# Attention in pairs of heads, with the stick-breaking weights from the sigmoid table

## The reference

```python
def nsa_compressed(q, kc, vc, slopes):       # 31 compressed keys
    ...
    p = jax.nn.softmax(s, axis=-1)
    p = jnp.where(valid.any(-1)[:, None], p, 0.0)
    o = jnp.einsum('bgrqn,bgnd->bgrqd', p.astype(vc.dtype), vc)
    return o, p.sum(axis=2)

def nsa_selected(...)   # s = q.k * scale - slope * dist, causal, softmax, times v
def nsa_window(...)     # the same with other keys and values

def stick_breaking(q, k, v):
    ...
        z = jnp.einsum('bhqd,bhkd->bhqk', qq.astype(jnp.float32), kf) * ATTN_SCALE
        log_keep = jnp.where(mask, -jax.nn.softplus(z), 0.0)
        later = lax.cumsum(log_keep, axis=3, reverse=True) - log_keep
        a = jnp.where(mask, jnp.exp(jax.nn.log_sigmoid(z) + later), 0.0)
        return jnp.einsum('bhqk,bhkd->bhqd', a.astype(v.dtype), v)

    o_a = g_a[..., 0:1] * o_cmp + g_a[..., 1:2] * o_sel + g_a[..., 2:3] * o_win
    y_a = o_a.transpose(0, 3, 1, 2, 4).reshape(B, S, NSA_Q_DIM) @ w_proj_a
    y_b = o_b.transpose(0, 2, 1, 3).reshape(B, S, SB_HEADS * hd) @ w_proj_b
    y = jax.nn.sigmoid(merge[:, :, 0]) * y_a + jax.nn.sigmoid(merge[:, :, 1]) * y_b
    return y @ w_out
```

## Time and profile before

| | us |
|---|---|
| median of 3 runs (2045.61 to 2047.15) | 2045.71 |
| profiled execution, its own time | 2046.02 |
| its span | 2044.3 |
| stage_compress, first instruction | 201.1 |
| attention's first instruction, first score | 264.9, 269.05 |
| first product of the merge | 435.53 |
| PE busy over the span | 1806.7 (88%) |
| DVE, ACT, POOL busy over the span | 819.3, 516.2, 36.1 |

### The profile page before, as it was taken

One profiled execution on the slowest core, in us unless ns is written; L12 is line 12 of the kernel. 1 busy time (PEld: TensorE's weight loads), 2 busy tenths in 40 slices (PEclk: granted clock), 3 DMA queues, 4 the chain that ended last, 5 costly groups with the idle time before them and its releaser, 6 DMA issues. The chain is left out here.

```text
span 2044.3 us, 20691 instructions
## 1 busy us (share of the span) xinstructions
PE 1806.7 (88%) x8271; PEld 1284.3 (63%) x8271; DVE 819.3 (40%) x1346; ACT 516.2 (25%) x873; POOL 36.1 (2%) x59
## 2 busy tenths in 40 slices
PE   6899779989987999999959989998899888888865
PEld 6788667766666888878848876757333343343344
DVE  1663388852225223233452274333423332322344
ACT  3312156641123222222243242322200000000032
POOL 0000000000000000000000000000200000000000
PEclk9899579999988999999979999999999999999977
DMA  8565100022331232230422111225599999999901
GB/s 330 178 242 182 43 1 1 1 83 70 136 124 41 84 123 83 87 120 21 165 72 83 42 42 41 83 115 240 193 427 424 427 427 426 427 427 427 424 18 41
DMA packets 93434, 353.71 MB, mean 173 GB/s; under 512 B 8813, under 2 KB 50457, under 8 KB 77593
## 3 DMA queue, kind: packets, MB, share of 16 engines
q1 hardware_dynamic: 90778, 343.98, 43.1%
q0 software_dynamic: 2560, 8.40, 1.1%
HBM read 343.93 MB, written 6.33 MB: 171 GB/s over the span
## 5 line engine op out<-in xcount | busy, mean ns | idle before, releaser
L549 PE MATMUL up_ps<-up_h,up_w 128*128 128x512 f32 x352 | 137.8, 391 | 5.7 <-DVE up_h L544 5.7
L544 DVE TENSOR_TENSOR p_w<-ring,p_w 128x1024 fp32r<-128x1024 f32 x60 | 73.5, 1224 | 167.1 <-ACT p_w L589 167.0
L550 PE MATMUL up_ps<-up_h,up_w 128*128 128x512 f32 x352 | 137.5, 391 | 0.0
L551 PE MATMUL up_ps<-up_h,up_w 128*128 128x512 f32 x352 | 137.4, 390 | 0.0
L2272 PE MATMUL ex_h<-ring,u_big_tail 128*64 128x512 f32 x512 | 116.6, 603 | 13.1 <-DMA ring<-in_w 12.5
L2272 PE MATMUL ex_h<-s_ab,u_big_tail 128*64 128x512 f32 x400 | 114.7, 596 | 12.6 <-DMA s_ab<-in_w 5.5
L589 ACT CAST p_w<-ring 128x1024 fp32r<-128x1024 f32 x60 | 62.8, 1047 | 128.7 <-PE p_ps L551 86.8
L2243 DVE TENSOR_TENSOR u_big_tail<-ex_x,vcol 128x512 f32<-128x512 f32 x32 | 20.6, 686 | 184.9 <-PE ex_x L2236 184.9
L544 DVE TENSOR_TENSOR up_w<-ring,up_w 128x1024 fp32r<-128x1024 f32 x44 | 53.9, 1226 | 87.1 <-ACT up_w L589 87.1
L2272 PEld LDWEIGHTS ex_h<-ring,u_big_tail 128*64 128x64 f32 x512 | 39.5, 138 | 76.0 <-issue 74.9
L2477 ACT ACTIVATE u_big_tail<-ex_h 128x512 f32<-128x512 f32 x16 | 9.6, 597 | 305.7 <-PE ex_h L2272 305.7
(11 more groups left out here) (484 smaller groups left out, 3772.2 us busy)
## 6 DMA issues: line engine op xcount, KB each, us to landing
ring<-in_w SPq DMA_DIRECT2D x48, 2048.0 KB, 28.8
s_ab<-in_w SPq DMA_DIRECT2D x36, 2048.0 KB, 28.3
ring<-in_w_in SPq DMA_DIRECT2D x15, 2048.0 KB, 9.0
reg_a<-in_w SPq DMA_DIRECT2D x12, 2048.0 KB, 32.4
ring<-in_w_ada SPq DMA_DIRECT2D x16, 1024.0 KB, 4.7
ring<-in_w_ffn_gate SPq DMA_DIRECT2D x11, 1024.0 KB, 5.2
ring<-in_w_ffn_up SPq DMA_DIRECT2D x11, 1024.0 KB, 7.8
ring<-in_w_ffn_down SPq DMA_DIRECT2D x5, 2048.0 KB, 7.7
```

What stands on the lines that cost most here:

```text
L544: return engine.tensor_tensor(lo, v, hi.bitcast(F32), ALU.subtract)
L549: nc.tensor.matmul(ps, x[0], y[0], start=start, stop=False)
L550: nc.tensor.matmul(ps, x[0], y[1], start=False, stop=False)
L551: return nc.tensor.matmul(ps, x[1], y[0], start=False, stop=stop)
```

## The change

Units become steps over pairs of heads: (block t, pair n, kind), first four stick pairs of a block, then eight softmax pairs, 48 in all. The query isn't spread any more: each head of the pair is a product over its own 64 rows. Each step's two heads lie in one buffer of two banks, `ps_s[i % 2]`, are copied in one instruction, and there is one transpose buffer `ps_t` of two banks. The stick weights are made from Sigmoid(-z), what is kept: ACT writes it (L1181), POOL writes 1 on and above the diagonal (L1226), DVE scans products from the right (L1150) and subtracts neighbours (L1153). The values are now the fixed operand (64 columns) and the turned weights move, so the outputs come with features on the partitions, head 2n in the lower and 2n+1 in the upper half; ACT copies them (L1187, L1191). Since tokens now lie along the columns, the factors of a block are widened by POOL (L1234), turned by eight products (L1099) in the next block's sixth step (`block_end(s, 6)`), copied by ACT (L1198), and DVE multiplies and adds (L1168 to L1170) into `b.qT`, from which the merge reads. The stick result goes into `b.sqT`. The turning stage is empty, and the reload of `b.reg_a` is issued at the attention's start. In stage_compress `b.sbmask` goes, `cs` is scaled by `cfac` before it is turned, and the product with the values is four products of 512 columns, copied by DVE and ACT in turn.

```diff
@@ stage_compress
-            nc.gpsimd.memset(b.sbmask, 0.0).then_inc(pool, 1)
-            pe.wait_ge(expd, 1)
+            pe.wait_ge(shared, 1)
...
-            for t in range(NT):
-                pe.wait_ge(pte, t // 2 + 1)
-                for g in range(2):
-                    mm = nc.tensor.matmul(ps_o[t][:, g * REP * HD:(g + 1) * REP * HD], pTc[:, t, g, :], vbd[:, g, :], ...)
+            pe.wait_ge(pte, 2)
+            for n in range(4):
+                nc.tensor.matmul(ps_o[n][:], vbd[:, n // 2, n % 2 * P:n % 2 * P + P], pTc[:, :, n // 2, :],
+                                 start=True, stop=True).then_inc(o, 1)
...
+            nc.vector.tensor_tensor(cs, cs, cfac.unsqueeze(3).to_broadcast([P, NT, HEADS, NC]), ALU.mult).then_inc(shared, 1)
@@ stage_attention
-    PER = 3 * HEADS
-    units = [(t, i // 3, i % 3) for t in range(NT) for i in range(PER)]
+    PER = 12
+    units = [(t, n, kind) for t in range(NT) for kinds in ((2,), (0, 1)) for n in range(4) for kind in kinds]
+        @block.sync
+            sp.dma_start(b.reg_a[:], b.h_dram).then_inc(b.h_back, 16)
         @block.tensor
+            def turn(i):      # waits p_stick or p_soft, and copied >= i
+                for e in range(2):
+                    for c in range(t + 1):
+                        mm = nc.tensor.transpose(ps_t[:, e, c * P:c * P + P], buf(i)[:, e, c * P:c * P + P], b.ident[:])
+                mm.then_inc(pt_ready, 1)
+            def values(i):    # waits copied >= i + 1
+                for c in range(t + 1):
+                    for e in range(2):
+                        mm = nc.tensor.matmul(ps_o[n % 2][64 * e:64 * e + 64, 0, kind * P:kind * P + P], v,
+                                              turned[i % 2][:, e, c * P:c * P + P], start=(c == 0), stop=(c == t))
+                    for e in range(2):
+                        r, k = slice(64 * e, 64 * e + 64), (t + 1) * P
+                        q = (b.sqT if kind == 2 else b.qT)[r, n, t * P:t * P + P]
+                        ks = b.skT[r, n, 0:k] if kind == 2 else b.kk[kind][r, n // 2, 0:k]
+                        nc.tensor.matmul(ps_s[i % 2][:, e, 0:k], q, ks, start=True, stop=True).then_inc(scored, 1)
+                if t is not None:                       # block_end(s, 6)
+                    pe.wait_ge(widened, 2 * t + 2)
+                    for kind in range(2):
+                        for n in range(4):
+                            mm = nc.tensor.matmul(ps_t[:, kind, n * P:n * P + P], wide[kind][:, n * P:n * P + P], b.ident[:], ...)
+                    mm.then_inc(spread, 1)
+                    values(at(s, 4)); pe.wait_ge(shared, t + 1); turn(at(s, 3))
+                else:
+                    turn(at(s, 3)); values(at(s, 4))
         @block.vector
+                    for e in range(2):                  # softmax pair, at its step
+                        nc.vector.tensor_tensor_reduce(out=buf(i)[:, e, 0:k], in0=ps_s[i % 2][:, e, 0:k], in1=b.bias[...], ...)
+                    for e in range(2):                  # stick pair, one step later
+                        last = nc.vector.tensor_tensor_scan(out=left[:, e, 0:k][:, ::-1], data0=w[:, e, 0:k][:, ::-1],
+                                                            data1=zero.to_broadcast([P, k]), initial=1.0, op0=ALU.mult, op1=ALU.add)
+                    nc.vector.tensor_tensor(w[:, :, 0:k], left[:, :, 1:k + 1], left[:, :, 0:k], ALU.subtract).then_inc(p_stick, 1)
+                    link(nc.vector.tensor_tensor(raw, raw, shares..., ALU.mult))      # block_end(s, 7)
+                    link(nc.vector.tensor_tensor(raw[:, 0], raw[:, 0], raw[:, 1], ALU.add))
+                    nc.vector.tensor_tensor(b.qT[:, :, q], raw[:, 0], b.oa[:, :, q], ALU.add).then_inc(y_made, 1)
         @block.scalar                                   # in this order within a step s
+                    nc.scalar.activation(buf(i)[:, :, 0:k], ps_s[i % 2][:, :, 0:k], ACT.Sigmoid, scale=-1.0)   # stick pair s
+                    last = nc.scalar.copy(b.sqT... or raw..., ps_o[n % 2]...)                                  # pair s - 5
+                    nc.scalar.copy(shares, ps_t[:]).then_inc(shared, 1)                                        # block_end(s, 6)
+                    nc.scalar.copy(turned[i % 2][:, :, 0:k], ps_t[:, :, 0:k]).then_inc(copied, 1)              # pair s - 3
+                    for e in range(2): nc.scalar.activation(buf(i)[:, e, 0:k], ..., ACT.Exp, ..., accum_out=...)  # softmax pair s
         @block.gpsimd
+                    nc.gpsimd.affine_select(out=own, in_=own, compare_op=ALU.is_gt, fill=1.0, base=0, ...)
+                        nc.gpsimd.tensor_copy(wide[kind]..., fac[:, :, kind].unsqueeze(2).to_broadcast([P, HEADS, HD]))
@@ stage_turn
+    return
```

More of the change, by code:

```diff
@@ L1024, in stage_attention, with pair @@
[L1024 to L1031 removed]
+    def pair(reg, u0):
+        return reg[:, u0 * U:(u0 + 2) * U].rearrange("p (e k) -> p e k", e=2)
@@ new lines, in stage_attention @@
+    turned = [pair(b.hTflat, 4 + 2 * i) for i in range(2)]
+    share = [pair(b.w1flat, 2 * i) for i in range(3)] + [pair(b.hTflat, 2 * i) for i in range(2)]
+    raw = b.w1flat[:, 6 * U:8 * U].rearrange("p (b n q) -> p b n q", b=2, n=4)
+    left = b.scr[:, 0:2 * U + 2].rearrange("p (e k) -> p e k", e=2)
+    wide = [b.scr[:, 2 * U + 2:3 * U + 2], b.u_big[:, 8 * U:9 * U]]
+    shares = pair(b.s_b, 4)
+    negm = b.small[:, 0:4].rearrange("p (i e) -> p i e", i=2)
+    fac = b.small[:, 24:40].rearrange("p (h b) -> p h b", b=2)
@@ new lines, in stage_attention, with stick, block_end, buf @@
+    first = [i for i in range(N) if units[i][2] != 1]
+    def stick(i):
+        return i is not None and units[i][2] == 2
+    def block_end(s, lag):
+        t = (s - lag + 1) // PER - 1
+        return t if (s - lag + 1) % PER == 0 and 0 <= t < NT else None
+    def buf(i):
+        return share[i % 5]
+    with ExitStack() as ps_ctx:
+        def banks(n, k):
+            return ps_ctx.enter_context(nc.psum_tensor(f"at_{n}", [P, k, CH], F32))
+        ps_s = [banks(f"s{i}", 2) for i in range(2)]
+        ps_t = banks("t", 2)
+        ps_o = [banks(f"o{i}", 1) for i in range(2)]
@@ L1077, in _ @@
[L1077 to L1087 removed]
+                    t, n, kind = units[i]
@@ new lines, in _ @@
+                i = at(s, 0)
+                if i is not None and not stick(i):
+                    t, n, kind = units[i]
+                    k, m = (t + 1) * P, softs.index(i)
+                    if t >= 2 and n == 0:
+                        act.wait_ge(fac_made, t - 1)
+                    for e in range(2):
+                        act.wait_ge(taken, 2 * m + e + 1)
+                        last = nc.scalar.activation(buf(i)[:, e, 0:k], buf(i)[:, e, 0:k], ACT.Exp, scale=-1.0,
+                                                    bias=negm[:, m % 2, e:e + 1], accum_out=b.rows2[:, t % 2, 2 * n + e, kind:kind + 1])
+                    last.then_inc(p_soft, 1)
```

346 lines of the change are left out of this document (139 added, 207 removed).

## The result

| | before | after |
|---|---|---|
| median, us | 2045.66 (2044.92 to 2047.15, 4 runs) | 2015.35 (2013.52 to 2018.86, 4 runs) |
| profiled span, us | 2044.3 | 2011.8 |
| first score of the attention | 269.05 | 269.65 |
| first product of the merge | 435.53 | 406.23 |
| between the two | 166.5 | 136.6 |

The account below looks back on a forecast made before the run. TensorE was taken to bound blocks t = 2 and 3. 267.5 + 117.0 + 7.5 + 1.5 + 15, + 2.5 - 0.5, put the merge at 410.5 against 435.5: 25 us less, 2045.7 to 2020.7 us, range 2005 to 2039.

Parts of the forecast that it names:

- PE's sum per step: Attention, PE's work per pair step with row halves at once: 1.20, 1.86, 2.51, 3.17 us for t = 0 to 3.
- The steps taken: Attention steps including waits between engines: 1.65, 2.15, 2.65 and 3.3 us, times 12 is 117.0 us.
- No successor to the stops: Block ends: PE's three old stops, 10.8 us in all, vanish; spreading the factors adds 2.5 us each, 7.5 us.
- t = 0: First attention block: ACT bounds it at 1.42 us a step, taken as 1.65; low clock at the start adds 1.5 us.
- First score: Attention's start: zeroing and copies go (-4.1 us), stage_compress grows; first score between 266 and 269.3, taken as 267.5 us.
- Tail: After the last step: transposes, copies, values, spreading, DVE steps and barrier take 15 us, where it was 20.
- Merge: Merge's first 3.7 us of products run at half speed for part of the time after PE idles: +2.5 us.
- (a): Rival, attention scores: row halves run one after the other, some 22 us more, 2043 us; chance 0.09.
- (b): Rival, softmax steps: PE's transposes, ACT's copy and two Exp follow without overlap, +14 us, 2034 us; chance 0.11.
- (c): Rival, attention: clock stays at 1.2 GHz because of PE's gaps, 47 us more if through t = 2, 2068; chance 0.06.
- (d): Rival, attention steps: everything overlaps as PE's sum alone, 12 us less, 2009 us; chance 0.08.
- (e): Rival, ACT: two heads in one instruction may cost more than one long row; ends in the ACT copy-loop rival, 2034.

Follow-up runs that it names:

- run 1: Changed kernel with both heads' score products reading the same upper 64 rows of queries and keys: 2038.93 us, ratio to before 0.9961.
- run 2: Changed kernel with transposes and value products reordered by head, adding two changes of shape in a step: 2028.57 us, 150.8 us from score to merge.
- run 6: Changed kernel with an exponential in place of the sigmoid, so no table loads within the attention: 127.9 us from score to merge; total 2364.12 us differs by its data.
- run 4: Changed kernel with five unread products of 512 columns on PE before the attention: 2010.94 us, ratio 0.9824, 136.4 us from score to merge.
- run 5: Kernel before the change, without DVE's wide steps at each block's end: 146.4 us from score to merge against 166.5; total 2094.0 us says nothing.
- run 11: Changed kernel with POOL's mask cut to 4 of 128 columns per head: 2084.88 us (differs by its data), 137.1 us from score to merge, single run.

## Why the prediction was right, point by point

2020.7 was forecast, 2015.35 measured; 25 us of gain, 30.3 measured. The main step, PE's sum with row halves at once, is right and shown. The total is closer than the parts deserve, by errors of opposite sign.

- *PE's sum per step*, 0.65(t+1) + 0.55, holds to 0.06 us: 1.86, 2.51, 3.17 against 1.81, 2.46, 3.11. Row halves at once: right (run 1). The switches, 0.55 a step from two gaps of the earlier trace rows, are 0.51, and 0.15 each when added (run 2). Two sums are a little off on paper: 120 records in 7.1 us are 0.059 each and not 0.055 (0.055 is their spacing inside that stretch), and 0.65 x 4 + 0.55 is 3.15, not 3.17.
- *The steps taken*, 2.15, 2.65, 3.3, added 0.13 to 0.29 for waits between engines. There are none in a steady step. That alone is 12 x (0.34 + 0.19 + 0.19) = 8.6 us too much.
- *"No successor to the stops" and table loads in ACT's sum alone*: wrong. The loads cost 6.2 us (run 6), as part of the spread's step and at each block's start. The spread itself costs 2.6, 2.5 and 2.1 us at t = 1 to 3 without its load (4.37 - 1.81, 4.99 - 2.46, 5.24 - 3.11), as taken. The two errors all but cancel, which is luck: 117.0 + 7.5 + 1.5 = 126.0 forecast for the four blocks, 122.2 measured.
- *t = 0* at 1.65 us and full from t = 1: the clock was at 0.61 through t = 0 and low until 298.0, the step 1.97. With the 1.5 us set aside, 21.3 forecast and 20.1 measured, though 12 steps of 1.97 would be 23.6: the first five steps, which lack values and in part transposes, take 6.2 us in all. The prediction had ACT as the bound of t = 0 at 1.42 us a step; ACT is busy for 13.6 of 20.1 us, and by run 1 the bound is PE at the low clock. Its sign for the clock, 0.95 or more from the second block on, failed too: t = 1 has 0.84. Its other signs held, with no stop of PE above 2.0 us and the merge 4 us before 410.
- *First score* 267.5, measured 269.65: 1.1 us of it lie before the change's code (the stage starts at 202.2 instead of 201.1), the rest in its four products, which ran low and took 5.9 us where run 4 has them in 3.7.
- *Tail* 15 (its parts add up to 14.0), measured 14.4. *Merge*: its first products took 5.4 us where they took 3.7, 1.7 for 2.5 forecast.
- *The gain that nothing in the sum explains*: of the profiled runs' 32.5 us, 3.2 come after the merge's start, where no instruction differs. The same stretch spreads over 10.5 us in the other kernels, so this can't be told from chance. The medians differ by 30.3, of which the merge's start accounts for 29.3 (435.53 to 406.23).

Of the rivals, (a) falls by run 1. (b) was named rightly for its place, ACT's copy, and wrongly for its form: the loop costs nothing in steady steps, only where a table load stands in it. (c) held in t = 0 and the start of t = 1; beyond that only 3.4 us of t = 2 were low. (d), to which 0.08 was given, is what the steady steps of t = 1 to 3 do: they are PE's sum alone. Its 2009 us missed by the loads and by the low clock of t = 0. (e) falls: ACT's copy of two heads at t = 3 takes 1.01 us, where 1.05 was taken. The larger omission is the other side of the sum: the forecast never said what the removal of the stops of the earlier trace rows, and of the low clock behind them, was worth by itself: up to 14.6 us, and 20 with the tail (run 5). Run 1's 24.8 us and these 20 don't add up to the change's gain; each is what one edit does with the other parts in place.

## What to carry over

Where one engine copies for another in a loop, a table load can be paid even if that engine is idle a fifth of the time (here 6.2 of 10.2 us). Count it on the path, and look whether the engine stands idle just ahead of the load. Here it does twice, for 1.85 us at t = 2 and 1.78 at t = 3, and not at t = 0 and 1. The next section shows why. To let the loads of t = 2 and 3 run within that idle time, as the one of t = 0 does, was not tried and is the next thing to try. When an edit of a few microseconds is judged, compare the distances between repeated instructions, not totals.

## What the hardware showed unexpectedly

- Two products from different halves of the rows run at once: four f32 records of 512 columns in 1.13 us, and in 1.98 us from the same half.
- A table load doesn't need its activation to be ready; what counts is which wait stands ahead of it. At the first softmax step of t = 0 the load begins 0.34 us before DVE has the minimum (275.75 and 276.09 us):

```profile
275.75 1.28 ACT L1214 ACT_TABLE_LOAD   x1
275.80 0.28 DVE L1134 CUSTOM_DVE_ANT_0 reg_b<-at_s,u_big 128x128 f32<-128x128 f32 x1
...
276.01 0.08 DVE L1134 DVE_READ_ACCUMULATOR2_ANT small<- 128x1 f32 x1
```

and in the earlier trace rows it ends 5 us before its exponential starts. At t = 2 and 3 it begins just after the minimum. The trace's semaphore records of ACT show the difference. At t = 0 and 1 the exponential itself carries the wait for the minimum, and the load runs ahead of it. At t = 2 and 3 the code gives this exponential a second wait (`fac_made`), which it then carries, and the wait for the minimum is a record of its own ahead of the load (368.01 us, the load at 368.06). The Trainium skill, "ScalarE: Activation LUTs", section "What ACT_TABLE_LOAD costs", puts 2.66 us on a switch, of which 1.28 are the load and 1.38 a drain. The rows agree on the load and don't show the drain: at t = 0 the load begins 0.02 us after ACT's copy has ended, and at t = 3 the activation starts 0.01 us after the load's end (368.06 + 1.28, 369.35).
- POOL and DVE take longer beside each other. The same mask, alone at the start of t = 3 and beside DVE's scans:

```profile
354.96 0.41 POOL L1226 TENSOR_SCALAR_AFFINE_SELECT w1flat<-w1flat 128x256 f32<-128x256 f32 x1 [26.97 <-ACT w1flat L1181]
...
363.72 1.32 POOL L1226 TENSOR_SCALAR_AFFINE_SELECT reg_b<-reg_b 128x256 f32<-128x256 f32 x1
```

and DVE's own scans of 512 columns in the changed kernel (count, busy us, mean ns):

```profile
L1150 DVE TENSOR_TENSOR_SCAN scr<-reg_b,small 128x512 f32<-128x512 f32 x4 | 5.1, 1304 | 0.1
```

With the small mask (run 11) this group is at 1264 ns and its twin at 1208 in the place of 1250, so the wide mask adds some 3% to DVE's scans (one run). That DVE's scans are what makes POOL's mask slow is read from when they meet, not tested; a rival for POOL's slow writes of factors, DVE's subtractions and scans at the same time, was not tried singly.
